# Output projection, second half: two of eight column pairs as seven block products, high casts and weighing moved to ScalarE, a new order on VectorE

## The reference, cut

```python
D_MODEL, SEQ, DEPTH, DEC_SEQ = 2048, 128, 2, 512        # 128 prompt tokens, 512 latent tokens, float32

def mixer_layer(x, mod, norm_w, w_in, ..., w_out, ctx):
    shift, scale, gate = jnp.split(mod, 3, axis=-1)
    xn = rmsnorm(x, norm_w) * (1.0 + scale[:, None, :]) + shift[:, None, :]
    proj = xn @ w_in
    ...
    mix = jnp.concatenate([out_a, out_b, out_c], axis=-1) @ w_out      # 2048 x 2048, the output projection
    x = x + gate[:, None, :] * mix
    return x, ...

# for l in range(DEPTH): one mixer_layer for the prompt and one for the latent tokens, with the same weights
y_prompt, y_sample = rmsnorm(h, final_norm_w), rmsnorm(z, final_norm_w)
```

## Time and profile before

| | before |
|---|---|
| median of 3 runs | 2118.37 us (2117.85 to 2119.13) |
| the profiled execution: its span | 2118.3 us |
| its own time beside that | none is listed: the page of this execution gives the span alone |
| TensorE busy | 2084.8 us, 98% |
| its weight loads | 1854.6 us, 88% |
| VectorE busy | 1487.4 us, 70% |
| ScalarE busy | 646.9 us, 31% |
| GpSimd busy | 173.2 us, 8% |
| HBM traffic | 172 GB/s |

### The profile page before, as it was taken

One profiled execution on the slowest core, in us unless ns is written; L12 is line 12 of the kernel. 1 busy time (PEld: TensorE's weight loads), 2 busy tenths in 40 slices (PEclk: granted clock), 3 DMA queues, 4 the chain that ended last, 5 costly groups with the idle time before them and its releaser, 6 DMA issues.

```text
span 2118.3 us, 33687 instructions
## 1 busy us (share of the span) xinstructions
PE 2084.8 (98%) x13031; PEld 1854.6 (88%) x13031; DVE 1487.4 (70%) x2921; ACT 646.9 (31%) x1100; POOL 173.2 (8%) x118
## 2 busy tenths in 40 slices
PE   5999999999999999999999999999999999999998
PEld 4788888888999999999998888888899999999998
DVE  5879789999666667866475455566666666677776
ACT  4232221311333334442043222232133333354312
POOL 0000000000000000523310000000000000043321
PEclk9999999999999999999999999999999999999999
DMA  9989687664333324664445647444343233266444
GB/s 365 388 303 341 211 282 261 233 222 161 115 106 104 106 71 130 201 208 142 128 129 166 189 127 216 144 143 146 109 128 107 74 101 107 86 213 214 149 120 154
DMA packets 357334, 365.43 MB, mean 173 GB/s; under 512 B 17670, under 2 KB 264156, under 8 KB 356572
## 3 DMA queue, kind: packets, MB, share of 16 engines
q1 hardware_dynamic: 328528, 320.67, 47.2%
q10 hardware_dynamic: 28684, 43.09, 5.4%
HBM read 304.98 MB, written 58.72 MB: 172 GB/s over the span
## 4 chain that ended last, share of the span: by engine, by line
PE 95%; DVE 2%; DMA 1%; issue 1%; ACT 0%; ACTq 0%; SPq 0%; DVEq 0%
PE psP L926 30%; PE psP L999 8%; PE psT L938 8%; PE psO L1008 7%; PE psP L996 6%; PE psP L994 6%; PE psP L995 6%; PE psP L1001 4%; PE psT L1008 4%; PE psP L1193 3%; PE psO L1239 3%; PE psT L1204 2%; PE psO L968 1%; DMA wmod<-in_w_mod_dram 1%; DVE r_a L2124 1%; PE psP L1056 1%
## 5 line engine op out<-in xcount | busy, mean ns | idle before, releaser
L926 PE MATMUL psP<-x_pair,high 128*128 128x512 f32 x1704 | 546.7, 391 | 0.0
L926 PEld LDWEIGHTS psP<-x_pair,high 128*128 128x128 f32 x1704 | 319.8, 188 | 70.5 <-issue 3.4
L926 PE MATMUL psP<-x_pair,low 128*128 128x512 f32 x852 | 331.8, 389 | 0.0
L1485 ACT ACTIVATE high<-raw 128x1024 fp32r<-128x1024 f32 x128 | 135.4, 1059 | 590.8 <-PE psT L938 504.2
L2025 DVE SCALAR_TENSOR_TENSOR macc<-mraw,cond,macc 128x128 f32<-128x128 f32 (+1 forms) x810 | 308.7, 455 | 0.0
L2043 DVE TENSOR_TENSOR low<-raw,high 128x1024 fp32r<-128x1024 f32 x128 | 157.1, 1228 | 172.9 <-ACT high L1485 172.8
L999 PE MATMUL psP<-x_pair,high 128*128 128x512 f32 x512 | 200.9, 392 | 0.0
L926 PEld LDWEIGHTS psP<-x_pair,low 128*128 128x128 f32 x852 | 160.0, 188 | 33.0 <-issue 0.5
L994 PE MATMUL psP<-x_pair,high 128*128 128x384 f32 x512 | 180.2, 352 | 0.0
L996 PE MATMUL psP<-x_pair,low 128*128 128x384 f32 x512 | 172.2, 336 | 0.0
L995 PE MATMUL psP<-x_pair,high 128*128 128x384 f32 x512 | 171.7, 335 | 0.0
(11 more groups left out here) (359 smaller groups left out, 4040.1 us busy)
## 6 DMA issues: line engine op xcount, KB each, us to landing
raw<-in_w_in_dram SPq DMA_DIRECT2D x132, 512.0 KB, 5.1
wmod<-in_w_mod_dram SPq DMA_DIRECT2D x32, 1024.0 KB, 8.6
mraw<-in_w_mod_dram SPq DMA_DIRECT2D x64, 512.0 KB, 4.2
mraw<-in_w_mod_dram SPq DMA_DIRECT2D x32, 1024.0 KB, 7.4
raw<-in_w_in_dram SPq DMA_DIRECT2D x32, 1024.0 KB, 5.5
raw<-in_w_out_dram SPq DMA_DIRECT2D x64, 512.0 KB, 4.0
old<-x_scratch SPq DMA_DIRECT2D x64, 320.0 KB, 2.9
xf<-proj_scratch SPq DMA_DIRECT2D x48, 320.0 KB, 3.3
```

The costliest lines, as they stand in the source:

```text
L926: mm = pe.matmul(latent_ps[m], own, moved, start=(k == 0 and w is whole and x is x_high), stop=(k == KT - 1 and x is x_low))
L1485: act.activation(ring(high, l, n), ring(raw, l, n), ACT.Copy).then_inc(s["chunk_cast"], 1)
```

## The change

**Seven block products.** In pairs 3 and 5 (`SEVEN_PAIRS`) the product of the pair's two weight tiles with the second half's tokens is done by a seven-product scheme for a 2 x 2 block product. The weight blocks are B11, B12, B21, B22: the first digit says even (1) or odd (2) k tiles, the second which output tile of the pair; a block is 4 k tiles of 128 columns, 512 elements per partition. The token blocks are A11, A12, A21, A22: the first digit says tokens 0 to 319 (1) or 320 to 639 (2), the second even (1) or odd (2) k tiles; 1280 elements per partition. Sums are made of both:

- weights ("block sums", L2826): T1 = B12 - B11, T2 = B22 - T1, T3 = B22 - B12, T4 = T2 - B21;
- tokens ("token sums", L2805): S1 = A21 + A22, S2 = S1 - A11, S4 = A12 - S2, S3 = A11 - A21. They are made once per layer.

The products are B11 x A11, B21 x A12, T2 x S2, T1 x S1, B22 x S4, T3 x S3, T4 x A22, in this order and called by their weight block. Each has 4 k steps of three matmuls with 320 columns (L1496), in seven half banks (`psP[0]`, `psO`, `psT`, `psP[1]`). Each block and each sum is split too: cast on ScalarE (L1986, L1971), low part on VectorE ("rest": L2831 for weights, L2810 for tokens). VectorE puts the products together in 13 short steps per pair ("joins", L2846 to L2880, of 320, 192 and 128 elements), ScalarE copies one product first (`corner_copy`, L1992).

**Plain pairs.** The other six pairs (`PLAIN`) are computed as before. Tile (p, j) is slot j of the p-th plain pair, p = 0 to 5. Pair 3 stands between (2,1) and (3,0), pair 5 between (3,1) and (4,0). Their high casts are now on ScalarE (L2011, `plain_cast`), the low parts L2784 (`split_plain`); the addition is `add_product`, now L2231 and L2235.

**Weighing.** In layer 1 tiles 0 to 13 are weighed by ScalarE (L2018); the last two stay on VectorE.

**SP** loads the first seven-product pair's weights early (`quad_weights(0)`), old x of both such pairs with two loads of 640 KB into `xf` (`kept_in`), and the second pair's weights (`quad_weights(1)`) when all seven rests of the first are made; the load for tile (3,1) stands behind these in SP's order.

Besides, the hardware loops of the stage are written out, and some semaphores are merged into others that count the same events. The squares (now L2001) and GpSimd's additions stay, one per tile.

```diff
+SEVEN = 7
+B11, B21, T2, T1, B22, T3, T4 = range(SEVEN)
+A11, A12, S2, S1, S4, S3, A22 = range(SEVEN)
+SEVEN_PAIRS = (3, 5)
+PLAIN = [i for i in range(OUT_PAIRS) if i not in SEVEN_PAIRS]
+WEIGHED = KT - 2
...
+                def quad_weights(m):
+                    for j in range(2):
+                        at = (2 * SEVEN_PAIRS[m] + j) * P
...
+                            sp.wait_ge(s["block_split"], weights_split(l, SEVEN * m))
+                        sp.dma_start(raw[j][:, HALF_K:, :], w_out[:, HALF_K:, at:at + P]).then_inc(s["quad_in"], 16)
...
+                quad_weights(0)
+                for n in range(1, PLAIN_PAIRS - 1):
+                    second_weights(1, n)
+                    sp.wait_ge(s["taken0"], n + occ + SECOND + SEED)
+                    old_x(0, PLAIN[n])
+                    second_weights(0, n + 1)
+                    sp.wait_ge(s["taken1"], n + occ + SECOND + SEED)
+                    old_x(1, PLAIN[n])
+                    if n == 2:
+                        kept_in(0)
+                        kept_in(1)
+                        quad_weights(1)
...
+                def seventh(m, idx):
+                    q, out = m * SEVEN + idx, product_banks[idx]
+                    pe.wait_ge(s["block_split"], weights_split(l, q + 1))
+                    if idx in (B11, T4):
+                        pe.wait_ge(s[f"taken{idx // T4}"], occ + SECOND + SEVEN_PAIRS[m] - m + SEED)
...
+                    for k in range(QUAD):
+                        for w, x in ((whole, x_whole), (whole, x_rest), (rest, x_whole)):
+                            mm = pe.matmul(out, w[:, k, :], x[:, k, :], start=(k == 0 and w is whole and x is x_whole),
+                                           stop=(k == QUAD - 1 and w is rest))
+                    mm.then_inc(s["product_done"], 1)
...
+                def plain_cast(p, j):
...
+                    act.activation(high[j][:, at:at + HALF_K], raw[j][:, 0:HALF_K], ACT.Copy).then_inc(s[f"high{j}"], 1)
...
+                def weigh(t):
+                    if l + 1 < DEPTH:
+                        return
+                    act.wait_ge(s["x_sq"], t + l * SQUARES + 1)
+                    act.activation(xf[:, t, :], xf[:, t, :], ACT.Identity, scale=head[:, 2 * KT + t:2 * KT + t + 1])\
+                        .then_inc(s["y_weighed"], 1)
...
+                plain_cast(1, 0)
+                token_cast(S1)
+                square(0, 0)
+                token_cast(S2)
+                plain_cast(1, 1)
+                weigh(0)
+                square(0, 1)
+                token_cast(S4)
+                plain_cast(2, 0)
+                weigh(1)
+                square(1, 0)
+                token_cast(S3)
+                quad_cast(B11)
+                quad_cast(B21)
+                plain_cast(2, 1)
+                weigh(2)
+                square(1, 1)
+                quad_cast(T2)
+                quad_cast(T1)
+                weigh(3)
+                square(2, 0)
+                quad_cast(B22)
+                quad_cast(T3)
+                weigh(4)
+                square(2, 1)
+                quad_cast(T4)
+                weigh(5)
+                corner_copy(0)
+                plain_cast(3, 0)
+                plain_cast(3, 1)
...
-                def finish(i, last=False):
-                    for f in range(3 if last else 4):
-                        after = i * 2 + (f + 1) // 2
-                        split_half(f + 1, after + (occ + SECOND), after + (whole + OUT_PAIRS))
-                        add_product(lambda part: xf[:, bass.ds(i * 4 + f, 1), part].rearrange("p a b -> p (a b)"),
-                                    psP[f % 2], f, i * 4 + f, i * 2 + (f // 2 + occ + SECOND),
-                                    i * 2 + (f // 2 + l * KT + OUT_PAIRS), i * 8 + 2 * (l * (KT - 1) + f + 1))
-                        if l + 1 == DEPTH and f > 0:
-                            weigh(i * 4 + (f - 1))
-                    if last:
-                        finish_last()
-                    elif l + 1 == DEPTH:
-                        weigh(i * 4 + 3)
...
+                def quad_summed(m, idx):
+                    dst, one, other = {T1: (first_sum, weight_block(0, 1), weight_block(0, 0)),
+                                       T3: (weight_block(0, 1), weight_block(1, 1), weight_block(0, 1)),
+                                       T2: (weight_block(0, 0), weight_block(1, 1), first_sum),
+                                       T4: (weight_block(1, 0), weight_block(0, 0), weight_block(1, 0))}[idx]
...
+                    dve.tensor_tensor(dst, one, other, ALU.subtract).then_inc(s["block_summed"], 1)
...
+                def quad_rest(q):
+                    dve.wait_ge(s["block_cast"], weights_split(l, q + 1))
+                    dve.tensor_tensor(weight_place(low, q), weight_source(q % SEVEN), weight_place(high, q).bitcast(F32),
+                                      ALU.subtract).then_inc(s["block_split"], 1)
...
+                def join(m, idx):
...
+                    elif idx == T2:
+                        dve.tensor_tensor(both, product, corner, ALU.add).then_inc(s["joined"], 1)
+                    elif idx == T1:
+                        dve.wait_ge(s["joined"], base + 3)
+                        dve.tensor_tensor(upper, product, both, ALU.add).then_inc(s["joined"], 1)
+                    elif idx == B22:
+                        dve.wait_ge(s["joined"], base + 4)
+                        dve.tensor_tensor(upper, product, upper, ALU.add).then_inc(s["joined"], 1)
+                        dve.wait_ge(s["joined"], base + 5)
+                        early(second, upper)
+                    elif idx == T3:
+                        dve.tensor_tensor(both, product, both, ALU.add).then_inc(s["joined"], 1)
+                        dve.wait_ge(s["joined"], base + 7)
+                        dve.tensor_tensor(lower, product_banks[T1], both, ALU.add).then_inc(s["joined"], 1)
+                        dve.wait_ge(s["joined"], base + 8)
+                        late(second, lower)
...
+                split_plain(0, 1)
+                token_summed(S1)
+                add_plain(0, 0)
+                split_plain(1, 0)
+                token_rest(S1)
+                token_summed(S2)
+                add_plain(0, 1)
+                split_plain(1, 1)
+                token_rest(S2)
+                token_summed(S4)
+                add_plain(1, 0)
+                split_plain(2, 0)
+                token_rest(S4)
+                token_summed(S3)
+                quad_summed(0, T1)
+                quad_summed(0, T3)
+                token_rest(S3)
+                quad_rest(B11)
+                quad_rest(B21)
+                split_plain(2, 1)
+                add_plain(1, 1)
+                quad_summed(0, T2)
+                quad_summed(0, T4)
+                quad_rest(T2)
+                quad_rest(T1)
+                add_plain(2, 0)
+                quad_rest(B22)
+                quad_rest(T3)
+                add_plain(2, 1)
+                quad_rest(T4)
+                for idx in range(SEVEN):
+                    join(0, idx)
+                    if idx == T2:
+                        split_plain(3, 0)
+                    if idx == B22:
+                        split_plain(3, 1)
+                quad_summed(1, T1)
+                quad_summed(1, T3)
+                quad_rest(SEVEN + B11)
+                quad_rest(SEVEN + B21)
+                quad_summed(1, T2)
+                quad_summed(1, T4)
+                quad_rest(SEVEN + T2)
+                quad_rest(SEVEN + T1)
+                add_plain(3, 0)
...
```

More of the change, by code:

```diff
@@ L1833, in square, with token_cast @@
                                    ACT.Square).then_inc(s["x_sq"], 1)
[L1835 to L1838 removed]
+                def token_cast(idx):
+                    act.wait_ge(s["block_summed"], tokens_summed(l, TOKEN_SUMS[idx]))
+                    act.activation(token_high[idx][:], token_sum(idx), ACT.Copy).then_inc(s["block_cast"], 1)
@@ new lines, in quad_cast @@
+                def quad_cast(q):
+                    m, idx = q // SEVEN, q % SEVEN
+                    before = occ + SECOND + SEVEN_PAIRS[m] - m
+                    if idx == B11:
+                        act.wait_ge(s["quad_in"], 32 * (l * len(SEVEN_PAIRS) + m + 1))
+                    if idx in WEIGHT_SUMS:
+                        act.wait_ge(s["block_summed"], weights_summed(l, m, WEIGHT_SUMS[idx]))
+                    if idx < 4:
+                        act.wait_ge(s["product_done"], l * PRODUCTS + SEVEN * m)
+                        act.wait_ge(s[f"tile_done{idx // 2}"], before - 1 + SEED)
+                    else:
+                        act.wait_ge(s[f"tile_done{idx // T4}"], before + SEED)
+                    act.activation(weight_place(high, q), weight_source(idx), ACT.Copy).then_inc(s["block_cast"], 1)
@@ new lines, in _ @@
+                weigh(3)
[9 more added lines that the diff above has]
```

(40 more changed lines are left out.)

348 lines of the change are left out of this document (242 added, 106 removed).

## The result

The change takes 2125.34 us (median of 7 runs, 2123.84 to 2129.78) against 2118.76 us before (7 runs): ratio 1.0032, 95% interval [1.0021, 1.0043]. It is slower by 0.3%, where "within 0.2%" was forecast at 2120; the time lies inside the range that was given, at its upper end.

The account below looks back on a forecast made before the run. The prediction took TensorE, busy 98% of the 2118.3 us span, as the bound. Over both layers, -6.3 saved, -0.6 late low parts and +8.8 waits gave +1.9 us, 2120.2, given as 2120; range 2112 to 2125.5.

Parts of the forecast that it names:

- TensorE's saving: Seven-product pairs take 12.3 us against 13.87 for a plain pair: 6.3 us saved for two pairs in two layers.
- late low parts: TensorE's three waits for VectorE's low parts in layer 1, 0.6 us in all, taken as gained.
- VectorE's prices: Start-to-start times on VectorE: low part 1.13 us, two-operand operation of 1280 elements 1.40, plain tile's addition 1.57.
- the port: VectorE and GpSimd block each other; a waiting GpSimd addition comes between back-to-back VectorE operations and costs VectorE 1.43 us.
- A cycle: VectorE's full round from the addition of (0,1) to that of (1,0): 7.73 us against TensorE's 6.935 per tile.
- First late place: Before tile (2,1): VectorE's addition of (1,1) hands over at 1011.5, TensorE is ready at 1009.7 and waits 1.8 us.
- Second late place: Before the second group's B11: VectorE's chain through the late (3,1) load ends at 1047.2; TensorE, there at 1044.6, waits 2.6 us.
- third load of the burst: SP's load for tile (3,1), queued behind the second group's two weight loads: lands after 7.0 us, bounds 4.6 and 8.0.
- the clock: TensorE's clock in the stage, read as 1.00 in both layers; the sum has no term for it.
- The base: The profiled execution's 2118.3 us, to which +1.9 us was added; said to agree with the median of 2118.37.
- The slower one: Rival: the chain before the second B11 grows, 1.2 us more per layer giving 2122.6 us, 2124.6 in all; chance 0.23.
- The one without a wait: Rival: no place in the stage is late, the saving is kept whole, 2111.4 us; chance 0.20.

Follow-up runs that it names:

- all three moves: The change with tile (0,1)'s cast before the store's issue, tile (3,1)'s load early and squares three tiles later: 2114.1 us, 0.9969 of the kernel before.
- Cast first: The change with ScalarE's cast for tile (0,1) ahead of the issue of the last old-x store: 2125.9 us, 1.0027 of the kernel before.
- the change again: The change unaltered, measured once more beside the kernel before in the same session: 2128.1 us, ratio 1.0041.
- other order: The change with the low part of (2,1) and addition of (1,1) ahead of seven block-work steps, ScalarE's order matched: 2129.7 us, 1.0052 of the kernel before.

## Why the prediction was wrong, point by point

- **TensorE's saving, 6.3 us: right.** The seven-product pairs take 12.31 us where nothing disturbs them, 12.3 forecast; 4 x (13.87 - 12.31) = 6.2. The 0.6 us of late low parts in layer 1 came to 0.5 (104.52 - 104.00; with all three moves both stages are 100.95).
- **VectorE's prices and the port: right.** A cycle takes 996.51 - 988.82 = 7.69 us, 7.73 forecast. GpSimd's block is in the first rest, 2.86 in place of 1.48 (1.38 us, where 1.43 was taken), and it comes three times before the addition of (1,1), on which (2,1) waits:

```profile
983.51 1.21 DVE L2784 TENSOR_TENSOR low<-raw,high 128x1024 fp32r<-128x1024 f32 x1
984.64 2.86 DVE L2810 TENSOR_TENSOR token_low<-xf,token_high 128x1280 fp32r<-128x1280 f32 x1
...
988.82 0.60 DVE L2231 SCALAR_TENSOR_TENSOR old<-psP,mod,old 128x128 f32<-128x128 f32 x2
...
996.51 0.60 DVE L2231 SCALAR_TENSOR_TENSOR old<-psP,mod,old 128x128 f32<-128x128 f32 x2
```

- **First late place: the failed step.** "From 982.2 it has the addition of (0,0)" took VectorE's first addition to start 7.3 us into the stage as before, with the low part of (0,1) made ahead of it. Its cast had moved to ScalarE, behind the issue of a store that waits for VectorE. ScalarE and VectorE there:

```profile
977.85 0.33 ACTq L1873 DMA_DIRECT2D x_scratch<-old  x1
978.30 2.01 ACT L2011 ACTIVATE high<-raw 128x1024 fp32r<-128x1024 f32 x2 [3.02 <-DVE old L2615]
```

```profile
979.40 1.22 DVE L2784 TENSOR_TENSOR low<-raw,high 128x1024 fp32r<-128x1024 f32 x1 [1.58 <-ACT high L2011]
980.54 1.48 DVE L2805 TENSOR_TENSOR xf<-xf 128x1280 f32<-128x1280 f32 x1
981.94 0.60 DVE L2231 SCALAR_TENSOR_TENSOR old<-psP,mod,old 128x128 f32<-128x128 f32 x2
```

  The low part starts 6.5 us into the stage (5.5 before, 980.44 - 974.90), the first sum follows it, and the addition starts at 9.0 (981.94 - 972.92), 1.7 us late. The prediction put this lateness at nothing. It cost 0.9 us before (0,1) and turned the forecast 1.8 us before (2,1) into 2.7. "Cast first" shows it: with the cast moved, the addition starts at 7.4 and the wait before (2,1) is 1.9 and 1.7. Over both layers it is 1.9 us before (0,1) and 1.8 before (2,1). From this addition on the working holds: to the end of the addition of (1,1) it had 29.2 us, and the trace shows 29.0 (1010.94, where VectorE's next step starts, less 981.94).
- **Second late place: right, in its chain and in its size over both layers.** 1.7 + 3.0 us and 0.1 by which what follows a wait is longer, 4.8 in all; 5.2 forecast. From the end of the addition of (1,1) to the burst 14.0 us were forecast and 13.9 measured (1024.80 - 1010.94); from ScalarE's use of the third load to TensorE's restart 14.8 and 14.7. What moved was the load between them. ScalarE used the third load of the burst 6.6 us (1031.44 - 1024.80) and 8.1 us (2049.71 - 2041.62) behind the burst's start, 7.0 forecast with 8.0 as the bound; its timeline:

```profile
1031.44 1.06 ACT L2011 ACTIVATE high<-raw 128x1024 fp32r<-128x1024 f32 x1 [7.16 <-DMA raw<-in_w_out_dram]
...
2049.71 1.06 ACT L2011 ACTIVATE high<-raw 128x1024 fp32r<-128x1024 f32 x1 [7.81 <-DMA raw<-in_w_out_dram]
```

  The forecast named the load, the squares ahead of the casts and GpSimd's additions as links of one chain, and it was so: taking out any one of the three removed the whole wait. Over all kernels with this burst the load was used 6.6 to 8.4 us behind it. How much later each further load of a burst comes, 1.5 us in the forecast, was an estimate, and no run measures it by itself.
- **The second term that failed: the clock, put at nothing.** The prediction read the clock as 1.00 in the earlier trace rows, where TensorE hardly waited, and had it stay so behind waits of 1.8 and 2.6 us. Low clock made the stage longer by 1.6 us in this profile, and by 3.2 in that of "the change again" and in that of "cast first". So mending the first cast alone does not bring the forecast time: "cast first" is at 2125.9.
- The sum by what the stage shows, each wait with the 0.1 us behind it: -6.2 - 0.5 + 1.9 + 5.4 + 4.8 + 1.6 = 7.0 us; 1.9 was forecast. Of the 5.1 us between them 3.7 are the late first cast and 1.6 the clock; the second place was 0.4 smaller, and the savings were 0.2 smaller. The base was misread besides: the span of 2118.3 and the median of 2118.37 were said to agree, but the span belongs to a time of some 2120.2. Between the two medians the change is 6.6 us, where 1.9 was forecast.
- **The rivals.** The slower one named the second chain; the time fell near its 2124.6, but that chain did not grow. The one without a wait needed "GpSimd's additions to fall into VectorE's waits", and that is what the squares moved by three tiles do: 2114.3 us, where it had 2111.4 from a base 0.5 to 1.1 us lower than the medians of the kernel before.
- What stays open: why the third load of the burst came 6.6 us behind it once and 8.4 another time; why the low clock came behind some waits of one length and not behind others; and why the wait before (0,1) varied between 0.1 and 0.8 us in layer 1. For the last the traces say only that VectorE's split of the tokens ahead of the stage began 2.0 us before TensorE's first tile where the wait is 0.8, and 2.7 where it is 0.1.

## What to carry to other kernels

When work moves to another engine, look up what stands ahead of it in that engine's order, a DMA issue that waits for a third engine included, and cost the first instruction of the stage as carefully as the loop. Where an engine's chain has no slack, as here, another order may only decide which wait pays; look for helpers of low urgency (here squares and their sums) that block it through a shared port or a shared queue, and put them where it waits anyway. A wait that several links feed can be removed at any one of them, so that an experiment which removes it has not shown the cause. When such a wait varies from run to run, measure the chain in pieces: here the pieces before and behind the load kept their length and the load did not.

## What the runs showed of the hardware

TensorE's clock fell to 1.2 GHz behind some of its waits, for some 3.6 us and a cost of 1.5 to 1.6 us, once for some 6 us and 2.8 ("other order", layer 1). In the ten profiles of kernels with the change it came behind all five waits of 2.7 us or more (2.7 to 3.3 us, by the table's measure), behind four of the nine of 2.6 to 2.7 us, behind the one of 2.2, and behind none of 2.0 us or less, of which there are more than a dozen. A stall of 2 to 3 us thus cost half as much again or more when it came.

A GpSimd addition of 640 elements and a VectorE operation of two SBUF operands that want the port together: VectorE's got longer by 1.4 us where it followed straight on another (the rest 2.86 for 1.48 in layer 0, in layer 1 also the sum, 2.85 for 1.48), and by 1.0 us where GpSimd had started 0.5 us earlier (two rests, 2.26 for 1.28). GpSimd's own addition took 1.6 to 2.7 us.
